# A fused transformer pair on one Trainium2 core: sums of a fast matrix product spaced four steps apart, one shift moved to VectorE, two token tiles modulated earlier

## What is computed

```python
def first_block(...):
    ...
    x = x + merged @ w_out[l]
    xn = rms_norm(x, ffn_norm_g[l])
    gate, up = jnp.split(xn @ w_gate_up[l], 2, axis=-1)
    x = x + (jax.nn.silu(gate) * up) @ w_down[l]      # D_FF = 2816
    return rms_norm(x, final_norm_g)

def second_block(...):
    hc = modulate(rmsnorm(ctx, norm1_g), csh1, csc1)  # 256 context tokens
    kv_c = hc @ w_in[:, 1024:1536]
    hx = modulate(rmsnorm(x, norm1_g), sh1, sc1)
    q_x, k_x, v_x, u_x, b_x, c_x, ga_x, gc_x = split_projection(hx @ w_in)
    ...
```

## Time and profile before

| | |
|---|---|
| median of three runs | 2991.09 us (2990.4 to 2992.05) |
| the profiled execution | 2991.9 us; its span 2990.1 us |
| PE busy | 2824.4 us, 94% of the span |
| DVE, ACT, POOL busy | 1825.1, 1332.8, 529.8 us (61%, 45%, 18%) |
| mean granted clock of PE | 0.975 |
| down product on PE | from 971.3 to about 1208 us of the span |

### The profile page before, as it was taken

The page is one execution under the profiler, slowest core; times in us unless marked ns, Lnnn a source line. Parts: engine busy times, 40 slices in busy tenths (PEclk is TensorE's granted clock), DMA queues, the critical chain, the costliest instruction groups (busy, mean ns, idle before and its releaser), DMA issues.

```text
span 2990.1 us, 34923 instructions
## 1 busy us (share of the span) xinstructions
PE 2824.4 (94%) x13918; PEld 2243.3 (75%) x13918; DVE 1825.1 (61%) x2521; ACT 1332.8 (45%) x1936; POOL 529.8 (18%) x435
## 2 busy tenths in 40 slices
PE   6999998999999989999999999999999479999996
PEld 5777777788778777888887667666888368888885
DVE  4344534788875577643233455554455669999997
ACT  4344433333233354221111666664223357777775
POOL 0011112555554020331000111111000200000000
PEclk9999999999999999999999999999999789999998
DMA  3210122345653986231211111115324569999996
GB/s 107 85 43 29 43 100 76 92 141 149 182 165 113 336 210 182 67 96 44 76 57 50 43 36 40 43 40 159 113 82 169 225 236 387 397 390 398 397 397 238
DMA packets 256549, 465.76 MB, mean 156 GB/s; under 512 B 28876, under 2 KB 135508, under 8 KB 255876
## 3 DMA queue, kind: packets, MB, share of 16 engines
q1 hardware_dynamic: 229712, 377.00, 36.1%
q0 software_dynamic: 26528, 86.50, 9.1%
q10 hardware_dynamic: 148, 0.04, 0.0%
HBM read 409.91 MB, written 53.58 MB: 155 GB/s over the span
## 4 chain that ended last, share of the span: by engine, by line
PE 83%; DVE 8%; DMA 4%; ACT 2%; issue 2%; POOL 1%; SPq 0%; ACTq 0%; POOLq 0%; DVEq 0%
PE PS L129 78%; PE PS L132 5%; DVE m L138 4%; DMA m<-h_scratch 2%; ACT m L135 2%; DVE m L144 1%; DMA m<-in_w_down_dram 1%; POOL m L138 1%; ACT L135 0%; DVE m L180 0%; DVE m L183 0%; DVE m L177 0%; DVE m L147 0%; SPq L186 0%; DVE m L141 0%
## 5 line engine op out<-in xcount | busy, mean ns | idle before, releaser
L129 PE MATMUL PS<-m,m 128*128 128x512 f32 (+6 forms) x12102 | 2637.7, 391 | 59.4 <-DVE m L138 35.6
L129 PEld LDWEIGHTS PS<-m,m 128*128 128x128 f32 (+3 forms) x12102 | 2039.4, 184 | 582.6 <-issue 121.3
L135 ACT ACTIVATE m<-m 128x512 fp32r<-128x512 f32 (+5 forms) x723 | 736.8, 1041 | 831.5 <-PE PS L129 434.9
L138 DVE TENSOR_TENSOR m<-m,m 128x512 fp32r<-128x512 f32 (+7 forms) x712 | 912.5, 1312 | 283.1 <-ACT m L135 214.4
L135 ACT ACTIVATE m<-PS 128x512 f32<-128x512 f32 (+4 forms) x507 | 281.9, 578 | 524.1 <-PE PS L129 346.0
L138 DVE TENSOR_TENSOR m<-PS,m 128x512 fp32r<-128x512 f32 (+1 forms) x356 | 233.6, 685 | 342.0 <-PE PS L129 300.6
L138 POOL TENSOR_TENSOR m<-m,m 128x512 f32<-128x512 f32 (+3 forms) x166 | 268.1, 1618 | 588.0 <-DVE small L147 207.9
L132 PE MATMUL PS<-ident,m 128*128 128x128 f32 x1592 | 226.1, 281 | 82.3 <-DVE m L153 35.9
L132 PEld LDWEIGHTS PS<-ident,m 128*128 128x128 f32 x1592 | 193.9, 145 | 121.3 <-DVE m L153 36.2
L135 ACT ACTIVATE m<-m,small 128x640 f32<-128x640 f32 (+4 forms) x199 | 156.3, 788 | 219.5 <-DVE small L141 154.0
L147 DVE CUSTOM_DVE_ANT_0 m<-PS,m 128x640 f32<-128x640 f32 (+4 forms) x192 | 146.5, 776 | 117.4 <-PE PS L129 117.4
(11 more groups left out here) (82 smaller groups left out, 484.8 us busy)
## 6 DMA issues: line engine op xcount, KB each, us to landing
m<-in_w_exp_gate_dram SPq DMA_DIRECT2D x64, 1024.0 KB, 8.4
m<-in_w_exp_up_dram SPq DMA_DIRECT2D x64, 1024.0 KB, 8.7
m<-in_w_exp_down_dram SPq DMA_DIRECT2D x64, 1024.0 KB, 8.1
m<-in_w_mod_dram SPq DMA_DIRECT2D x48, 512.0 KB, 3.8
m<-in_w_gate_up_dram SPq DMA_DIRECT2D x44, 512.0 KB, 6.5
m<-in_w_in_dram SPq DMA_DIRECT2D x41, 512.0 KB, 4.0
m<-in_w_in_dram SPq DMA_DIRECT2D x12, 1024.0 KB, 5.0
h_scratch<-m POOLq DMA_DIRECT2D x22, 512.0 KB, 3.6
```

The lines of the kernel that those rows point to most:

```text
L129: return Unsent() if self.e is None else self.e.matmul(o, l, r, start=first, stop=last, **k)
L135: return Unsent() if self.e is None else self.e.activation(o, i, fn, **k)
L138: return Unsent() if self.e is None else self.e.tensor_tensor(o, a, b, op)
```

## The change

Five edits. (1) The order in the place aside: T3's first chunk goes behind the three of S2 (`ASIDE`, `down_sp`). (2) The steps after which DVE sums, `sums`: S1 13, 17, 21 (12, 15, 18 before), S3 first 25 (23), S2 29, 32, 35 (28, 31, 34), T3 first 39 (25), S3 second 42 (37), T3 second 45 (40), S3 third 48 as before, T3 third 51 (50). (3) SP's list: S1's second and third chunk behind ring loads 21 and 23 (19 and 21 before), S3's first behind 29 (25), and the large load of A21 (2816 KB) before ring load 10 instead of 11. (4) The shift of the context is added by DVE, after steps 40 and 41, and PE turns it behind steps 68 to 71 (70 to 73 before). (5) DVE scales tiles 5 and 6 inside P3 (after steps 74, 76); in the second block tile 7 comes first, the result C12 before the low parts of V2, and the square sums of tiles 0 to 3 and their mean and root are spread out.

```diff
@@ -1575,7 +1575,7 @@
             sp.dma_start(w_slot[s_], w_block(b, t, 1)).then_inc(*sp.landed(f"wd_in{s_}", "d", j))
 
 
-        ASIDE = [("S1", 0), ("S1", 1), ("S1", 2), ("S3", 0), ("T3", 0), ("S2", 0), ("S2", 1), ("S2", 2),
+        ASIDE = [("S1", 0), ("S1", 1), ("S1", 2), ("S3", 0), ("S2", 0), ("S2", 1), ("S2", 2), ("T3", 0),
                  ("S3", 1), ("T3", 1), ("S3", 2), ("T3", 2)]
 
         def aside_load(sp, S, c):
@@ -1612,28 +1612,27 @@
         def down_sp(sp):
             sp.wait_ge("gu_acc", 21, "P7")
             sp.dma_start(t_all, blocks(w_block("B12", 0, 11))).then_inc(*sp.landed("ct_in"))
-            for j in range(8, 22):
-                if j == 11:
-                    sp.wait_ge("gu_acc", 21, "P4")
-                    sp.wait_ge("gu_up", 21, "C12")
-                    sp.wait_ge("h_st0", 20)
-                    sp.wait_ge("h_st1", 21)
-                    sp.dma_start(s_all, blocks(h_block("A21", 0, 11))).then_inc(*sp.landed("cs_raw"))
-                if j in (14, 20):
-                    aside_load(sp, "S1", (14, 20).index(j))
+            for j in range(8, 10):
+                h_ring_load(sp, j)
+                w_ring_load(sp, j)
+            sp.wait_ge("gu_acc", 21, "P4")
+            sp.wait_ge("gu_up", 21, "C12")
+            sp.wait_ge("h_st0", 20)
+            sp.wait_ge("h_st1", 21)
+            sp.dma_start(s_all, blocks(h_block("A21", 0, 11))).then_inc(*sp.landed("cs_raw"))
+            for j in range(10, 24):
+                if j in (14, 22):
+                    aside_load(sp, "S1", (14, 22).index(j))
                 h_ring_load(sp, j)
                 w_ring_load(sp, j)
             aside_load(sp, "S1", 2)
-            for j in range(22, 26):
+            for j in range(24, 30):
                 h_ring_load(sp, j)
                 w_ring_load(sp, j)
             aside_load(sp, "S3", 0)
-            for j in range(26, 30):
-                h_ring_load(sp, j)
-                w_ring_load(sp, j)
-            aside_load(sp, "T3", 0)
             for c in range(3):
                 aside_load(sp, "S2", c)
+            aside_load(sp, "T3", 0)
             aside_load(sp, "S3", 1)
             aside_load(sp, "T3", 1)
             aside_load(sp, "S3", 2)
@@ -1699,10 +1698,10 @@
                             pe.take(b, *(("dn_s1", i) if P == "P1" else ("x2_half", DN_TAKEN[P], i)))
                         mm3(pe, PS[:, b, :], (ah[:, tile128(i)], al[:, tile128(i)]), (bh, bl), t == 0 and not added, t == 10,
                             **(dict(skip_group_check=True) if added else {})).then_inc(*pe.did("dn_acc", n, i))
-                    if P == "P3" and 4 <= t < 8:
-                        _, a, k0 = md_parts[t - 4]
+                    if P == "P3" and 2 <= t < 6:
+                        _, a, k0 = md_parts[t - 2]
                         pe.wait_ge("cx_shifted", a)
-                        pe.turn = t - 4
+                        pe.turn = t - 2
                         turn4(pe, cx[:, a, :], k0, 4, "md_turned", ("c", a, k0), ("md_low", md_no["c", a, k0]))
             pe.turn = 0
 
@@ -1852,7 +1851,6 @@
                     dn_squares(act, 0, (n - 26, n - 25))
                 if n == 36:
                     act.wait_ge("cx_in")
-                    act.wait_ge("x2_half", "T3", 0)
                     for a in range(2):
                         for z in range(2):
                             square(act, cx[:, a, half512(z)], ssqc[:, a, z:z + 1], "cx", a, z, junk=ar(94, 512))
@@ -1988,8 +1986,8 @@
                     dve.tensor_tensor(xs, xs, PS[:, i + 4, :], ALU.subtract).then_inc(*dve.did("x2_half", "C12", i))
 
         def down_dve(dve):
-            sums = {4: ("T1", 0), 5: ("T1", 1), 11: ("T1", 2), 12: ("S1", 0), 15: ("S1", 1), 18: ("S1", 2), 23: ("S3", 0),
-                    25: ("T3", 0), 28: ("S2", 0), 31: ("S2", 1), 34: ("S2", 2), 37: ("S3", 1), 40: ("T3", 1), 48: ("S3", 2), 50: ("T3", 2)}
+            sums = {4: ("T1", 0), 5: ("T1", 1), 11: ("T1", 2), 13: ("S1", 0), 17: ("S1", 1), 21: ("S1", 2), 25: ("S3", 0),
+                    29: ("S2", 0), 32: ("S2", 1), 35: ("S2", 2), 39: ("T3", 0), 42: ("S3", 1), 45: ("T3", 1), 48: ("S3", 2), 51: ("T3", 2)}
             results = {24: "C11", 46: "U2", 48: "U2_in", 57: "U3", 58: "U3_in", 59: "C22", 62: "U3_in0", 68: "C21"}
             for n in range(4, 77):
                 dn_lows(dve, n)
@@ -2011,6 +2009,10 @@
                     for a in range(2):
                         dve.scalar_tensor_tensor(cx[:, a, :], cx[:, a, :], rsc[:, a:a + 1], cA1row, ALU.mult, ALU.mult).then_inc(
                             *dve.did("cx_scaled", a))
+                if n in (40, 41):
+                    a = n - 40
+                    dve.wait_ge("cx_scaled", a)
+                    dve.tensor_tensor(cx[:, a, :], cx[:, a, :], csh1row, ALU.add).then_inc(*dve.did("cx_shifted", a))
                 if n == 50:
                     w_low(dve, W_K2)
                 if n in (64, 66):
@@ -2025,7 +2027,8 @@
                     modulate_dve(dve, 4)
                 if n >= 73:
                     md_low(dve, *md_parts[n - 73], hch, hcl)
-            modulate_dve(dve, 5)
+                if n in (74, 76):
+                    modulate_dve(dve, n // 2 - 32)
 
         def row_load(pool, dst, j, c, sem):
             src = rows_dram[j:j + 1, 1024 * c:1024 * c + 1024]
@@ -2084,10 +2087,6 @@
                 *pool.landed("x1_back", "second"))
             for c in range(3):
                 dn_add(pool, "T4", c)
-                if c == 0:
-                    for a in range(2):
-                        pool.wait_ge("cx_scaled", a)
-                        pool.tensor_tensor(cx[:, a, :], cx[:, a, :], csh1row, ALU.add).then_inc(*pool.did("cx_shifted", a))
             for c in range(3):
                 dn_add(pool, "S4", c)
             pool.wait_ge("x1_back", "second")
@@ -2294,12 +2293,13 @@
             act.wait_ge("kc_acc", 0)
             act.activation(kc[:, 0, :], ps("kc_acc", 0)[:, 0:256], ACT.Copy).then_inc(*act.did("kc_out_a"))
             md_highs(act, "x", 4, hxh)
-            dn_squares(act, 1, range(4))
+            dn_squares(act, 1, range(2))
             v2_evacuate(act, 0)
             md_highs(act, "x", 5, hxh)
-            h2_root(act, 0)
+            dn_squares(act, 1, range(2, 4))
             for i in (6, 7):
                 md_highs(act, "x", i, hxh)
+            h2_root(act, 0)
             rope_act(act, rope_list[0])
             v2_evacuate(act, 6)
             md_highs(act, "x", 0, hxh)
@@ -2321,21 +2321,22 @@
                     rope_act(act, t)
 
         def second_dve(dve):
+            dn_result(dve, "C12")
             w_low(dve, W_V2)
-            dn_result(dve, "C12")
-            modulate_dve(dve, 6)
+            modulate_dve(dve, 7)
             dve.wait_ge("kc_acc", 1)
             dve.tensor_copy(kc[:, 1, :], ps("kc_acc", 1)[:, 0:256]).then_inc(*dve.did("kc_out_v"))
             md_lows(dve, "x", 4, hxh, hxl)
-            modulate_dve(dve, 7)
-            for i in range(4):
+            for i in range(2):
                 h2_sum(dve, 1, i)
-            h2_mean(dve, 0)
             md_lows(dve, "x", 5, hxh, hxl)
             v2_evacuate(dve, 1)
+            for i in range(2, 4):
+                h2_sum(dve, 1, i)
             md_lows(dve, "x", 6, hxh, hxl)
+            md_lows(dve, "x", 7, hxh, hxl)
+            h2_mean(dve, 0)
             h2_inverse(dve, 0)
-            md_lows(dve, "x", 7, hxh, hxl)
             modulate_dve(dve, 0)
             modulate_dve(dve, 1)
             rope_dve(dve, rope_list[0])
```

4 lines of the change are left out of this document (2 added, 2 removed).

## The result

| | before | changed |
|---|---|---|
| median of 14 runs each | 2991.97 us (2990.4 to 2996.48) | 2997.89 us (2995.71 to 3001.83) |
| ratio of the times, 95% interval | | 1.0018, 1.0009 to 1.0026 |
| the profiled execution, its span | 2991.9, 2990.1 us | 2995.71, 2993.9 us |

A forecast was written before the change was run, and what follows sets the result against it. PE, busy 94% of the span, was taken as the bound, with only its idle time and lower clock to win or lose. Terms 7.5 + 1 - 2.5, plus 0.5 for A21, gave +6.5: 2997.6 us, range 2985 to 3004.

The forecast's parts named there:

- the two new stalls: PE's down product: about 7 us at step 44 and about 10 us at step 49, neither there before.
- Ring loads 20, 21; A21: Loads ahead of S1's second chunk: step 18 2.7 us earlier; A21 one ring pair earlier costs +0.5.
- S3's first chunk: Behind ring load 29 it delays step 26, so the 2.7 us gained are gone again (bounds -3.5 and +2).
- Step 33: S2's sums at 29, 32, 35: the stall moves from 29 to 33, 2 us instead of 2.39; net 0.
- The shift, -6.1: Shift on DVE removes step 40's 3.57 us stall and 2.5 us at the lower clock: -6.1 by step 44.
- Rival C: Shift did not hold step 40, T3's second sum did; stall stays: +6.1, 3003; chance 0.08 with worse.
- Step 44: Chain of single chunks makes a new stall of about 7 us, giving back the 6.1: +0.4 against before.
- Step 49: S3's third chunk and ring loads starved by S4's adds: new stall of about 10 us, start at 1137.5.
- Rival A: S4's adds do not starve SP's queue; step 49 loses 1 to 3 us: about 2989 to 2992; chance 0.17.
- The sum: Lag by step 51: +0.4 + 10.1 - 3.0 (old stall at 51 gone) = +7.5.
- The lower clock, +1: Behind the second new stall the lower clock costs 2 to 3 us against 2 before: +1.
- The second block, -2.5: About 2 of the 4.02 us stall go, perhaps some lower clock behind it: -2.5 (bounds 0 and -6).

The follow-up runs named there:

- e5: Changed kernel with S4's accumulating adds issued only after S3's third sum and behind x_scratch's last row; 2986.07 us, 0.9976 of the kernel before.
- e6: Changed kernel with T3's second sum behind step 47 instead of 45, so behind U2's parts on DVE; 2998.18 us, 1.0019 of the kernel before.
- e7: Changed kernel with ring loads 30 and 31 ahead of S3's third chunk in SP's queue; 2989.11 us, 0.9983 of the kernel before.
- e3: Kernel before with the new order and spacing of sums and loads only, without ACT's wait for T3's first sum; 3002.07 us, ratio 1.0038.
- e1: Kernel before with only the context's shift moved to DVE after steps 40 and 41; 2991.0 us, ratio 1.0000.
- e12: Changed kernel with S4's adds late, S3's first chunk behind ring load 25, and the shift back on POOL; 2983.87 us, 0.9969 of the kernel before.
- e2: Kernel before with only tiles 5 and 6 scaled inside P3 and the second block's new order; 2991.19 us, ratio 0.9993.
- e4: Kernel before with the shift on DVE and the second block's new order, without the spacing; 2989.74 us, ratio 0.9991.
- e10: Kernel before with the shift on DVE, the second block's new order and S4's adds late, sums in old places; 2981.28 us, ratio 0.996.

## Why the prediction was right, and where its steps were not

Size and sign were right (2997.6 forecast, 2997.89 measured), and the two new stalls stand where it put them, with their causes shown by e5, e6 and e7. That it is right to 0.3 us is luck: the base, 2991.09, was 0.9 us under the median of 14 runs, and the down product and the second block were off by 2.9 and 1.6 us in opposite ways. By its steps, each time after its own step 0 (the forecast's less 971.27):

- **Ring loads 20, 21; A21.** Step 18 came 2.8 us earlier than before (forecast 2.7); its stall is 1.98. Step 11 came 0.1 us earlier, the +0.5 for A21 was not there.
- **S3's first chunk.** Its sum starts at 80.6 us (forecast 79.7) and step 26 at 84.2 (forecast 83.3), 0.7 us later than before. "Gone again" held, and e3 shows the reason: where T2's first add meets less of the chunk's load, the sum starts near the lower bound (76.5 us, bound 76.1).
- **Step 33.** No stall; the forecast had 2 us. PE came later than forecast, with 3.1 us lost at the lower clock behind step 26 (52.13 us for 49.0); e3, which lost nothing there, has 2.35 us at step 33.
- **The shift, -6.1.** This is the step that failed. Alone it gave 0 (e1), since T3's second chunk came next and later, in the old order as well; in the new order it shortens the chain by 2.3 us (e3) to 2.8 (e12). Rival C named that very chunk, with the stall of step 40 staying, and was right of the shift alone; it was wrong in adding the lost 6.1 to the new stalls. They are for the most part one wait (4.09 + 4.04 for 7.95), and the credit and the debit of 6 to 7 us were the same microseconds twice. It did no harm to the sum, because step 44 was taken from the end of the chain, which does not use the credit.
- **Step 44.** Forecast 142.3 us, measured 144.2, so +2.3 against before where +0.4 stood. T3's second sum begins 1.8 us later than forecast.
- **Step 49.** Forecast a stall of 10 us and a start at 166.2; measured 9.95 and 170.0, so +13.9 against before for 10.1. Of the 3.8 us the chain brought 1.7, and the loads 2.1 (22.2 us from 1111.36 to S3's third sum, for 20.1). SP's share was forecast as 0.106 MB/us and measured as 0.108. Rival A is out.
- **The sum.** "+0.4 + 10.1 - 3.0" counts the 0.4 twice, since 10.1 is step 49 against before and holds it: it should be 7.1.
- **The lower clock, +1.** Right: behind step 49 it cost 3.3 us, behind 51 before 2.2. The 3.1 us behind step 26 and the 2.2 behind 44 add nothing, because the waits at 44 and 49 end with the loads and swallow them, as the prediction said of the first of its two stalls. So at the end of the last product the lag was 264.4 - 252.6 = +11.9 after step 0 (the 16 transposes at 1233.45 and 1223.82), which is 13.9 - 3.0 + 1.0, where the terms gave 9.0: it is step 49 that was sized 3.8 us too small.
- **The second block, -2.5.** Measured 1.63 of stall and 2.47 of lower clock, -4.1. The stall's part came in every trace with the edit. Up to 1.6 of the other is luck of this execution: behind the same stall e2, e4, e6 and e7 take some 15.7 us where it takes 14.05. Together +7.8 for the stretch, +6.5 forecast, and 5.4 by the ratio of the times.

**Rule and row.** The prediction read the even turn of the Trainium skill (DMA: Bandwidth & Descriptors, section on queues, rings and completion order) as an even share of the free rate, 0.19 MB/us. The DMA queues of the changed kernel, first from 1118 to 1131 us, where both have work all the time, then from 1109 to 1115, where q0 has the adds alone:

```profile
q0 software_dynamic: 883, 1.90, 71.5%
q1 hardware_dynamic: 883, 1.64, 38.1%
```

```profile
q0 software_dynamic: 621, 1.24, 112.6%
```

883 packets each: counted in the trace's packets (most have 2048 bytes; whether they are the page's packets no run shows) the turns are even, as the page says. What is not even is the time of a turn. In the first window a packet of q0 holds an engine for 0.715 x 16 x 13 / 883 = 0.168 us, one of SP's for 0.090. Alone the adds move 1.24 MB in 6 us, 0.207 MB/us, with all engines full (packets of one engine overlap a little, hence the 112.6%), where plain loads had 0.386; together the two queues move 3.54 MB in 13 us, 0.272, and SP's queue has 0.126 of it. The 0.108 of the 20 us from 1113 on (and the 0.106 of the earlier trace rows, as far as its window is alike) is less, because at its start SP's queue moved nothing: its loads were issued from 1111.36 on, and q1 has no packet from 1109 to 1115. So even turns give SP's queue nearly half (1.64 MB to 1.90) of a slower total, and not of the free rate.

**What is open.** That T2's first add makes the stall at step 26 is read from five traces that differ by chance; no run moved that add by itself. Why the spacing with the adds late (e5) stays behind the old order (e10) is read from stalls only (6.58 at step 26, 8.77 at 44); no run took its three edits singly.
